# A second merge on 32x32 tiles, its blocks spread by GpSimd, and VectorE's convolutions placed behind the merges

## The reference

```python
qkv = silu(causal_depthwise_conv(qkv, conv_w))          # 4 taps
beta = sigmoid(b); g = -exp(a_log) * softplus(a + dt_bias)
# chunks of 64 positions, per head
gc = cumsum(g)
decay = where(causal, exp(min(gc_i - gc_j, 0)), 0)
m = where(strict, (k * beta) @ k.T * decay, 0)
t_inv = triangular_solve(eye + m, eye)                   # inverse of a unit lower triangle
u = t_inv @ (v * beta);  w = t_inv @ (k * beta * exp(gc))
qk = where(causal, q @ k.T * decay, 0)
# over the chunks: v_new = u - w @ state; o = qg @ state + qk @ v_new; state = state * exp(g_last) + kd.T @ v_new
o = rms_norm(o, o_norm) * silu(z)
out = o @ w_out
```

## Time and profile before

| | |
|---|---|
| median of 3 runs | 3183.93 us (3171.11 to 3185.95) |
| profiled execution: its time, its span | 3190.3 us, 3188.6 us |
| TensorE busy | 3048.5 us, 96% |
| VectorE, ScalarE, GpSimd busy | 70%, 53%, 26% |
| granted TensorE clock, mean | 0.989 |
| load of one weight block of 1 MB in the DeltaNet stage, issue to landing | 5.9 us |

### The profile page before, as it was taken

How to read it: one execution, slowest core, us unless ns; L and a number is a source line. 1 busy time by engine, 2 the same in 40 slices (tenths; PEclk the granted TensorE clock), 3 DMA queues, 4 the chain that set the end, 5 groups by cost and what they waited for, 6 DMA issues and landing times.

```text
span 3188.6 us, 68087 instructions
## 1 busy us (share of the span) xinstructions
PE 3048.5 (96%) x21974; PEld 2662.1 (83%) x21974; DVE 2231.3 (70%) x4305; ACT 1705.7 (53%) x3775; POOL 826.2 (26%) x1418
## 2 busy tenths in 40 slices
PE   5999999999989999999999999999999999999998
PEld 4888888888878888888888887888888888888887
DVE  5767676767755788667887767886677654776566
ACT  5565656565554555444555556764555544555444
POOL 1000000000010488888888810770000000000000
PEclk8999999999999999999999999999999999999999
DMA  6444445444467777877777866785766677667765
GB/s 166 120 131 122 126 123 135 123 125 122 134 173 184 200 201 203 227 198 200 206 210 203 212 189 166 231 255 145 184 184 185 188 185 185 183 185 185 185 159 141
DMA packets 1036180, 556.46 MB, mean 175 GB/s; under 512 B 38192, under 2 KB 1023952, under 8 KB 1035584
## 3 DMA queue, kind: packets, MB, share of 16 engines
q1 hardware_dynamic: 969088, 491.18, 58.0%
q10 hardware_dynamic: 58160, 37.63, 4.0%
q0 software_dynamic: 8848, 26.59, 2.7%
HBM read 528.30 MB, written 27.03 MB: 174 GB/s over the span
## 4 chain that ended last, share of the span: by engine, by line
PE 66%; DVE 16%; ACT 8%; issue 8%; DMA 1%; ACTq 1%; DVEq 1%; POOL 0%; SPq 0%; POOLq 0%
PE bank L308 36%; PE bank L309 19%; DVE w_lo L292 6%; ACT w_hi L286 3%; DVE y L1781 2%; PE bank L305 1%; ACT T L947 1%; PE bank L306 1%; DVE tiles L1965 1%; DVE normed L1977 1%; DVE tiles L334 1%; PE bank L639 1%; ACT L947 1%; PE bank L804 1%; ACT dec L947 1%
## 5 line engine op out<-in xcount | busy, mean ns | idle before, releaser
L292 DVE TENSOR_TENSOR w_lo<-raw,w_hi 128x512 fp32r<-128x512 f32 x1856 | 1297.7, 751 | 144.7 <-ACT w_hi L286 136.5
L308 PE MATMUL bank<-act,w_hi 128*128 128x512 f32 x3376 | 1227.5, 405 | 21.9 <-DVE w_lo L292 10.4
L309 PE MATMUL bank<-act,w_lo 128*128 128x256 f32 x4352 | 1224.5, 281 | 0.0
L308 PE MATMUL bank<-mid,w_hi 128*128 128x512 f32 x3072 | 1088.5, 399 | 3.7 <-DVE w_lo L292 2.8
L286 ACT ACTIVATE w_hi<-raw 128x512 fp32r<-128x512 f32 x1856 | 1039.2, 620 | 68.1 <-PE bank L309 43.7
L309 PE MATMUL bank<-mid,w_lo 128*128 128x256 f32 x3072 | 861.9, 281 | 0.0
L309 PEld LDWEIGHTS bank<-act,w_lo 128*128 128x128 f32 x4352 | 827.8, 190 | 0.8
L308 PEld LDWEIGHTS bank<-act,w_hi 128*128 128x128 f32 x3376 | 637.5, 189 | 179.2 <-DVE w_lo L292 14.2
L308 PEld LDWEIGHTS bank<-mid,w_hi 128*128 128x128 f32 x3072 | 578.3, 188 | 146.4 <-issue 3.4
L309 PEld LDWEIGHTS bank<-mid,w_lo 128*128 128x128 f32 x3072 | 581.5, 189 | 0.2 <-issue 0.2
L324 ACT ACTIVATE tiles<-bank 128x256 f32<-128x256 f32 x323 | 123.3, 382 | 540.5 <-PE bank L309 536.2
(11 more groups left out here) (344 smaller groups left out, 2939.6 us busy)
## 6 DMA issues: line engine op xcount, KB each, us to landing
raw<-in_mlp_w_up_dram SPq DMA_DIRECT2D x128, 1024.0 KB, 6.3
raw<-in_mlp_w_down_dram SPq DMA_DIRECT2D x128, 1024.0 KB, 6.2
raw<-in_gdn_w_in_dram SPq DMA_DIRECT2D x96, 1024.0 KB, 5.9
raw<-in_gdn_w_out_dram SPq DMA_DIRECT2D x32, 1024.0 KB, 6.5
raw<-in_ple_w_gate_dram SPq DMA_DIRECT2D x32, 1024.0 KB, 6.3
raw<-in_s_w_out_dram SPq DMA_DIRECT2D x28, 1024.0 KB, 6.7
raw<-in_s_w_in_dram ACTq DMA_DIRECT2D x10, 1024.0 KB, 6.6
c_scratch<-c_pow ACTq DMA_DIRECT2D x32, 256.0 KB, 4.3
```

The lines of the kernel that those rows point to most:

```text
L292: eng.tensor_tensor(w_lo[par][:, c], raw[slot][:, c], w_hi[par][:, c].bitcast(F32), ALU.subtract).then_inc(S("lo_ready"), 1)
L308: eng.matmul(a[:, :], w_hi[par][:, w], rhs[:, k0 + kt, :], start=(k0 + kt == 0), stop=False)
L309: mm = eng.matmul(a[:, 0:NT], w_lo[par][:, w], rhs[:, k0 + kt, 0:NT], start=False, stop=(k0 + kt == kend - 1))
```

## The change

The second merge works on 32x32 tiles: step 6 reads the band `pr[:, :, 1, :]` in place of `RT`, and step 7 reads `dm32`, the band transposed, and a new tile `wt2`. GpSimd copies the band's blocks to `RT`'s diagonal and two blocks of `dm32` to `Dm`, for the third merge. `RT` is cleared once before the rounds. Steps 8 and 9 use 64 rows of their operands. VectorE's two value convolutions, the decay products and the gates come after the merges. `low` runs two quarters later in the program than before: `low(-2)` and `low(-1)` are the former `low(22)` and `low(23)`, and `low(20)` and `low(21)` stand behind the subtraction into `mid`. TensorE's value transposes go from step 8 to 10 and the value steps from 10 to 14 go to 12 to 16, with ScalarE's pieces; step 16's goes to 17.

```diff
                 elif s == 6:
                     w("RT_ready", 7, 5)
+                    pe.sem_inc(S("tiles_begun"), 1)
                     for m in range(4):
-                        mm = pe.matmul(A[0:96, 64 * m:64 * m + 64], Mp[:, m, 0:96], second_half(RT, m), start=True, stop=True)
+                        for j in range(2):
+                            near, far = slice(64 * j, 64 * j + 32), slice(64 * j + 32, 64 * j + 64)
+                            mm = pe.matmul(A[near, 32 * m:32 * m + 32], Mp[far, m, near], pr[far, m, 1, :], start=True, stop=True)
                     mm.then_inc(S("X_done"), 1)
                 elif s == 7:
                     w("Dm_ready", 3, 2)
                     w("WT_ready", 3, 2)
+                    pe.sem_inc(S("tiles_begun"), 1)
                     for m in range(4):
-                        mm = pe.matmul(C[0:96, 64 * m:64 * m + 64], Dm[:, m, 0:96], packed(WT, m), start=True, stop=True)
+                        for j in range(2):
+                            near = slice(64 * j, 64 * j + 32)
+                            mm = pe.matmul(C[near, 32 * m:32 * m + 32], dm32[near, m, :], wt2[near, m, :], start=True, stop=True)
                     mm.then_inc(S("R_done"), 1)
                 elif s == 8:
                     w("RT_ready", 7, 6)
+                    w("RT_spread")
+                    pe.sem_inc(S("tiles_begun"), 1)
                     for m in range(4):
-                        mm = pe.matmul(A[0:64, 64 * m:64 * m + 64], Mp[:, m, 0:64], RT[:, m, 64:128], start=True, stop=True)
+                        mm = pe.matmul(A[0:64, 64 * m:64 * m + 64], Mp[64:128, m, 0:64], RT[64:128, m, 64:128], start=True,
+                                       stop=True)
                     mm.then_inc(S("X_done"), 1)
+                elif s == 9:
+                    w("Dm_ready", 3, 3)
+                    w("Dm_spread")
+                    w("WT_ready", 3, 3)
+                    pe.sem_inc(S("tiles_begun"), 1)
+                    for m in range(4):
+                        mm = pe.matmul(C[0:64, 64 * m:64 * m + 64], Dm[0:64, m, 0:64], packed(WT, m)[0:64], start=True, stop=True)
+                    mm.then_inc(S("R_done"), 1)
+                elif s == 10:
...
                     w("X_done", 3, 2)
-                    A_(fl(WT)[0:96, 0:NT], A[0:96, 0:NT]).then_inc(S("WT_ready"), 1)
+                    A_(fl(wt2)[0:96], A[0:96, 0:P]).then_inc(S("WT_ready"), 1)
                 elif s == 7:
+                    se.wait_ge(S("RT_cleared"), 1)
                     w("R_done", 4, 3)
                     for j in range(2):
-                        mm = A_(RT[64 * j:64 * j + 32, :, 64 * j + 32:64 * j + 64], by_half(C)[64 * j:64 * j + 32, :, j, :], scale=-1.0)
+                        mm = A_(RT[64 * j:64 * j + 32, :, 64 * j + 32:64 * j + 64], by_head(C)[64 * j:64 * j + 32], scale=-1.0)
                     mm.then_inc(S("RT_ready"), 1)
                 elif s == 8:
                     w("X_done", 3, 3)
                     A_(fl(WT)[0:64, 0:NT], A[0:64, 0:NT]).then_inc(S("WT_ready"), 1)
+                elif s == 10:
                     w("kv_turned", 2, 2)
                     for m in range(4):
                         mm = A_(Vb[:, m, :], Dk[:, m * P:(m + 1) * P], scale=col(H_BHALF + m))
...
-                elif s == 3:
-                    gate_tanh(n + 2, 0, y[:, 2, :], "conv_done", 4 * r + 3)
                 elif s == 4:
                     half_copy(se, n + 5, n + 4, 0)
-                elif s == 6:
+                elif s == 8:
+                    gate_tanh(n + 2, 0, y[:, 2, :], "conv_done", 4 * r + 3)
+                    half_copy(se, n + 6, n + 5, 1)
+                elif s == 9:
                     gate_tanh(n + 3, 1, y[:, 3, :], "conv_done", 4 * r + 4)
-                elif s == 8:
-                    half_copy(se, n + 6, n + 5, 1)
+                elif s == 10:
                     gate_tanh(n + 4, 0, z[:, 0, :], "acc_freed", n + 5)
                     if last:
                         gate_tanh(n + 5, 1, z[:, 1, :], "acc_freed", n + 6)
                 if last:
                     return
-                if s == 10:
+                if s == 11:
                     gate_tanh(n + 5, 1, y[:, 0, :], "conv_done", 4 * r + 5)
...
-                    if s in (10, 13):
+                    if s in (9, 10, 12, 15):
...
-            with gp.Fori(1, KH) as r:
+            gp.wait_ge(S("RT_cleared"), 1)
+            with gp.Fori(0, KH) as r:
                 gp.wait_ge(S("kk_done"), r + 1)
-                gp.sem_inc(S("RT_read"), 1)
-                gp.memset(RT[0:32, :, 32:64], 0.0).then_inc(S("RT_cleared"), 1)
-                gp.memset(RT[64:96, :, 96:128], 0.0).then_inc(S("RT_cleared"), 1)
-                gp.memset(RT[0:64, :, 64:128], 0.0).then_inc(S("RT_cleared"), 1)
+                gp.sem_inc(S("Dm_free"), 1)
+                gp.memset(Dm[0:32, :, 32:64], 0.0).then_inc(S("Dm_cleared"), 1)
+                gp.wait_ge(S("Dm_cleared"), r + 1)
+                gp.wait_ge(S("RT_ready"), 7 * r + 5)
+                gp.sem_inc(S("spread_begun"), 1)
+                for j in (2, 3, 0, 1):
+                    whole = gp.tensor_copy(block_32(RT, j), pr[32 * j:32 * j + 32, :, 1, :])
+                whole.then_inc(S("RT_spread"), 1)
+                gp.wait_ge(S("RT_spread"), r + 1)
+                gp.wait_ge(S("Dm_ready"), 3 * r + 2)
+                gp.sem_inc(S("spread_begun"), 1)
+                for j in range(2):
+                    whole = gp.tensor_copy(block_32(Dm, j), dm32[32 * j:32 * j + 32])
+                whole.then_inc(S("Dm_spread"), 1)
...
-                low(0)
                 spread(1, pr[:, :, 0, :])
-                low(1)
+                low(-2)
                 spread(2, pr[:, :, 0, :])
                 add_to_R(1, A)
-                low(2)
+                low(-1)
+                low(0)
                 spread(3, pair_of(C, 0))
                 add_to_R(2, C)
-                conv(r, n + 2, 2)
-
-                w("qk_done")
-                qk = B[:, 0:256].rearrange("p (b q) -> p b q", b=2).unsqueeze(2).to_broadcast([P, 2, 2, P])
-                bh = lambda a: a[:, :, :].rearrange("p (b h) q -> p b h q", b=2)
-                TT(bh(qkT), bh(dec), qk, ALU.mult).then_inc(S("qk_decay"), 1)
-                low(3)
-                w("qk_decay")
-                TT(qkT[:, :, :], qkT[:, :, :], U.unsqueeze(1).to_broadcast([P, 4, P]), ALU.mult).then_inc(S("qkT_ready"), 1)
+                low(1)
                 w("R_done", 4, 1)
                 w("RT_ready", 7, 3)
                 TT(pr[:, :, 1, :], pair_of(A, 0), pr[:, :, 1, :], ALU.add).then_inc(S("RT_ready"), 1)
                 w("RT_ready", 7, 4)
                 ve.transpose(dm32[:, :, :], pr[:, :, 1, :]).then_inc(S("Dm_ready"), 1)
+                low(2)
+                sum_halves(ve, n + 4, 0, z[:, 0, :], 2 * r + 3)
+                low(3)
+                w("R_done", 4, 2)
+                w("Dm_ready", 3, 1)
+                STT(pr[:, :, 1, 16:32], C[:, 0:64].rearrange("p (m q) -> p m q", m=4), tcol[:, 2:3], pr[:, :, 1, 16:32],
+                    ALU.mult, ALU.add).then_inc(S("RT_ready"), 1)
+                w("RT_ready", 7, 5)
+                ve.transpose(dm32[:, :, :], pr[:, :, 1, :]).then_inc(S("Dm_ready"), 1)
+                low(4)
+                low(5)
+                conv(r, n + 2, 2)
+                w("RT_ready", 7, 6)
+                ve.transpose(Dm[32:64, :, 0:32], RT[0:32, :, 32:64]).then_inc(S("Dm_ready"), 1)
+                low(6)
+                conv(r, n + 3, 3)
+                gate(n + 2, 0, y[:, 2, :])
+                low(7)
+                sum_halves(ve, n + 5, 1, z[:, 1, :] if last else pre[:, 0, 3:NT + 3], 2 * r + 4)
+                gate(n + 3, 1, y[:, 3, :])
+                w("qk_done")
+                qk = B[:, 0:256].rearrange("p (b q) -> p b q", b=2).unsqueeze(2).to_broadcast([P, 2, 2, P])
+                bh = lambda a: a[:, :, :].rearrange("p (b h) q -> p b h q", b=2)
+                TT(bh(qkT), bh(dec), qk, ALU.mult).then_inc(S("qk_decay"), 1)
+                if not last:
+                    low(8)
+                w("qk_decay")
+                TT(qkT[:, :, :], qkT[:, :, :], U.unsqueeze(1).to_broadcast([P, 4, P]), ALU.mult).then_inc(S("qkT_ready"), 1)
                 w("erow_ready")
                 w("qkn_ready")
                 TT(qeT[:, :, :], qkn[:, 1:2, :].to_broadcast([P, 2, P]), erow[:, :, :], ALU.mult).then_inc(S("qeT_ready"), 1)
-
-                low(4)
-                sum_halves(ve, n + 4, 0, z[:, 0, :], 2 * r + 3)
-                gate(n + 2, 0, y[:, 2, :])
-                conv(r, n + 3, 3)
-                low(5)
-                w("R_done", 4, 2)
-                w("Dm_ready", 3, 1)
-                STT(pr[:, :, 1, 16:32], C[:, 0:64].rearrange("p (m q) -> p m q", m=4), tcol[:, 2:3], pr[:, :, 1, 16:32],
-                    ALU.mult, ALU.add).then_inc(S("half_merged"), 1)
-                w("half_merged")
```

(46 more changed lines are left out.)

2 lines of the change are left out of this document (removed).

## The result

The changed kernel takes 3214.81 us, median of 4 executions (3208.9 to 3217.7), against 3183.49 for the kernel before on the same chip (4 executions, 3171.11 to 3185.95). The ratio is 1.0104, 95% interval 1.0074 to 1.0134: slower by 1.0%, and outside the predicted range. The profiled execution took 3208.9 us (span 3207.2), against 3190.3 (3188.6).

The account below looks back on a forecast made before the run. TensorE, busy 93 of 100 us in this stage, was taken as the bound. Its waits and work summed to 52.26 against 51.74 us a round, +0.52 over 15 rounds, +8: 3192 us, range for all cases 3174 to 3206.

Parts of the forecast that it names:

- Next: `low(20)`: Round's end: `low(20)` behind key matrix and `mid` makes TensorE wait 2.1 us at the next step 0; 1.95 lost.
- The walk: Bookkeeping of one DeltaNet round, engines in program order: 44.33 us to `qkn` plus 7.93 to the next step 0, 52.26.
- the old order: The same bookkeeping applied to the kernel before: 51.74 us a round, against 51.55 in the trace.
- The last round and what follows: Last round: first value product at 22.8 us after step 0 against 22.9 before, so 0 change.
- The forecast's own range: Bounds of steps 6 to 9 and of the tax: 0 to +1.0 us a round, 3184 to 3199.
- No wait ahead of steps 1, 4 and 6: TensorE's merges: with convolutions, decays and gates behind them these waits go; 3.2 us of waiting gone.
- No tax: VectorE's two-input operations beside GpSimd's copies: slowdown taken as 0, bounds 0 and 0.4 us a round.
- Step 13's wait: TensorE at step 13 waits 1.6 us for weights from `low(9)`, done at 26.2 against 24.8.
- the state's: Step 14's product waits 0.56 us for ScalarE's state copy, behind a tanh that waits for the sixth convolution.
- (a): Rival: VectorE keeps up, TensorE doesn't wait at step 0; 50.9 us a round, -13 us, 3171; chance 0.15.
- (b): Rival: GpSimd's copies slow and taxing VectorE; +17 us (3201), or +37 (3221) at 1.5 a copy; chance 0.20.
- (c): Rival: orders cancel, leaving TensorE's lighter work; 51.35 to 51.74 a round, 3178 to 3184; chance 0.15.

Follow-up runs that it names:

- `e1_low20_back`: The changed kernel with `low(20)` and `low(21)` back ahead of the key matrix: 3172.32 us, 0.9953 of the kernel before.
- `e2_low20_late`: The kernel before with only `low(20)` and `low(21)` moved behind the `mid` subtraction: 3207.55 us, ratio 1.0072.
- `e7_filled_wait`: The changed kernel with four products on constants put into TensorE's wait at step 0: 3195.7 us, 1.0026 of the kernel before.
- the second measurement: The changed kernel, unaltered, run again later on one chip with other kernels: 3209.42 us, 1.0081 of the kernel before.
- `e4_copies_twice`: The changed kernel with GpSimd's six copies made a second time, into a spare tile: 3211.25 us, 1.0074 of the kernel before.
- `e3_merge_alone`: The kernel before with the second merge on 32x32 products and GpSimd's spread, VectorE's order kept: 3165.76 us, ratio 0.9938.
- `e6_low9_alone`: The changed kernel with `low(9)` right behind the mask of `qkT`, `low(20)` still late: 3193.59 us, 1.0032 of the kernel before.

## Why the prediction was wrong

**What failed: the step *Next: `low(20)`* and the sum it went into.** It prices the wait at its length with TensorE at the 2.4 GHz level throughout. The wait came nearly as forecast (1.93 for 2.1). But TensorE's clock fell behind it in every second round, about 1.4 us each. Undoing the move removes both (`e1_low20_back`), the move alone brings both (`e2_low20_late`), and filling the wait removes the falls and leaves the wait (`e7_filled_wait`). The Trainium skill, "TensorE: Matmul & The Clock Gate", section "A second HAM failure mode: psum-queue depth-cycling", tells of short, frequent idle times between groups of matmuls that make the clock swing between its two levels. The traces agree that idle time between groups of products can be followed by the low level; here it is one wait of 1.93 us a round, not many short ones. I had the clock of 1.00 from 300 to 400 us before me and took it for the whole stage, though the change made a wait longer than any in the round I walked. The trace of the kernel before held the sign: its clock fell three times behind a wait of 1.6 us, and two of these falls made a round of 53.11 us, which is why the average of 51.7 lies above the 51.55 of the walked one.

The falls are not the whole miss. They are 5.4 of the 10.6 us by which the profiled execution missed, and the median missed by 23.

**The sum, term by term.** In the profiled execution I forecast +8 and it was +18.6:
- The walk itself held. From step 0 to `qkn` 44.36 us (135.60 to 179.96) for 44.33, from `qkn` to the next step 0 7.87 (to 187.83) for 7.93: a round of 52.23 for 52.26.
- Its value for the old order, 51.74, was 0.18 above the true 51.56. I had seen that the trace gave 51.55 and subtracted the bookkeeping from the bookkeeping all the same, in the belief that the error is common to both orders. It isn't: the new order's bookkeeping was right to 0.03, the old one's off by 0.18, +2.2 us in 15 rounds.
- The falls: +5.4 net of those that the kernel before had.
- The last round and what follows, forecast at 0: +4.7, of which 2.4 by the first product on `mid`; the cause of the rest is open. The opening -1.6.

Sum: 8 + 2.2 + 5.4 + 4.7 - 1.6 = 18.7.

The forecast's own range was narrower than its bounds: 0.52 + 0.35 (second merge free of gain) + 0.1 + 0.4 is 1.4 a round, 3204 instead of 3199. The result lies above that too.

**Between profile and median.** The medians differ by 31 us, and by 25 in the second measurement, while the profiled executions differ by 19 and 21. In the second measurement the kernel before scatters over 18 us (3174.5 to 3192.5). In the first its profiled execution, which is none of the four, lay 7 above their median; the changed kernel's profiled one lay 6 below its own. What makes an execution of the same program 10 us longer, no run here tells. This part stays open, and no term of my sum could have caught it.

**Steps that held.** No wait ahead of steps 1, 4 and 6; 21.0 us from step 0 to the value transposes forecast, 471.71 - 450.56 = 21.15 in `e7_filled_wait`, where no fall disturbs it. Step 6's products take 0.37 us to the next start (465.93 to 466.30), for 0.38. GpSimd's copies take 0.47 and 0.53 us for 0.45, hidden. No tax: `low` means 687 ns for 684. Step 13's wait is 1.3 for 1.6, and the state's 0.27 for 0.56. Two `low` stand right behind `mid`, and the period is 52.2 in rounds without a fall.

**The rivals.** (a), no wait at step 0, fell. `e1_low20_back` comes nearest to its case by an edit: 14.8 us under the kernel before, for 13. The round is 50.33 for 50.9; the prediction doesn't show where its 50.9 comes from (52.26 less the wait of 2.1 would be 50.2), so that the times agree is in part luck. (b), GpSimd slow, fell by its own rows (copies of 0.47 and 0.53 us) and by `e4_copies_twice`. (c), that the orders cancel, fell too: the round without a fall is 52.23, not 51.35 to 51.74, and what the merge wins (1.3 a round, `e3_merge_alone`) is given away by the order with something on top. What was missing is a rival that TensorE itself becomes slower.

**Where the change's gain went.** The merge and the spread win 1.3 us a round. The new place of `low(20)` takes 50.33 against 52.83 on average (792.47 / 15), 2.5 a round: 1.9 of waiting and 0.6 of low clock. VectorE's other moves win nothing by themselves: with them 50.33, without them 50.26 (`e1_low20_back`, `e3_merge_alone`), for most of what the waits at steps 1, 4 and 6 cost is now waited for at step 13 and the state (1.3 and 0.3). They pay only when `low(9)`, the state copy and the tanh follow: 49.27, then 48.27.

## What to carry to other kernels

In a round in which two engines feed a third, a work item moved back costs its lateness at the place where it is wanted, so list for each moved item the step that reads it and the time at which its reader gets there; taking one move of the reordering back was worth 2.5 us a round here, more than any other edit. When an edit makes TensorE wait longer than it did at any point of the loop, forecast a case in which its clock falls, with the price from rows at either level; look at the granted clock over the whole stage, before and after, and not in one stretch of it. Harmless products put into such a wait tell the two costs apart in one run.

## What the hardware did that I had not expected

- A wait of 1.93 us once in 52 us was followed by 3.4 us at the 1.2 GHz level in every second round of the changed kernel from its third on, in ten rounds of `e2_low20_late`, and in every third round of `e6_low9_alone`. A wait of 1.60 us was followed by such a fall in three of 16 rounds of the kernel before. With the longest wait in the rounds at 1.3 us (`e1_low20_back`) and at 1.0 us (`e3_merge_alone`) there was none. In the kernel before a wait of 2.00 us at 912.37 was followed by none either.
- What decides between equal waits is open. The length alone doesn't. The place of the wait in time may; no run here moved it by itself.
- In the rounds no fall began during the wait. It began 0.6 to 0.9 us after the weights started in the changed kernel (450.10, then 450.88), 0.4 to 1.5 in `e2_low20_late`, and about 1.6 behind the wait in the kernel before. In the last round of the changed kernel it began with the wait, after two shorter ones.
- GpSimd's copies of 32x128 beside VectorE at 68% cost VectorE nothing that shows: `low` 687 ns with GpSimd at 6%, 688 with the copies doubled, while it was 920 ns with GpSimd at 85%.
